# Front of a one-core hybrid encoder step: input blocks taken in threes, and the first B tile projected chunk by chunk behind the dt tile

## The chip, the core and the metric

The kernel runs on one core of one Trainium2 chip. The metric is the device time of the whole program in microseconds. The core's engines are TensorE (PE, matrix products and transposes), VectorE (DVE), ScalarE (ACT), GpSimd (POOL) and SyncE (SP), which issues the transfers. Each runs its own instructions in order, and they meet at semaphores.

## The reference, cut to what matters

The program is two layers over 1024 prompt tokens and 32 sample tokens of width 1024. Only the front of the even layer is touched:

```
h = rmsnorm(x, g_pre)                        # 1056 tokens, mean square over 1024
proj = einsum('bld,de->ble', h, w_in)        # columns: u, v, za, zb, xbc, dt_raw
xbc = silu(causal_dwconv(xbc))               # 12 tiles of 128 columns: x (8), B (2), C (2)
dt = softplus(dt_raw + dt_bias)              # 16 heads
acs = cumsum(dt * a)  per block of 128       # decays of the state recurrence
```

The recurrence, the gating branch, the output projection and the attention layer that follow are the same in both kernels.

## The kernel before, in words

**Layout.** The hidden state h is kept transposed: `HH` and `HL` are [128, 8, 1056], feature within tile, tile k, token. `HH` is h rounded to the matmul's input type and `HL` is the rest, so that a product is three matmuls: WH with HH, WH with HL, WL with HH. `WRAW`, `WH` and `WL` have two slots, so weight tile w uses slot w mod 2. A weight tile is loaded by SP into `WRAW`, rounded by ScalarE (`split_high`, to `WH`), and its rest is taken by GpSimd (`split_low`, to `WL`, counted by `w_low`). The tokens are projected in three chunks c of 352 columns, each into its own bank PB[c]. One chunk of one tile is 8 k-steps of 3 matmuls, 24 in all (`project_chunk`). ScalarE then reads the bank (`read_chunks`, counted by `c_read0` to `c_read2`), and only then may TensorE write the next tile's chunk there.

**Making h.** For each block of 128 tokens: a square with a row sum on ScalarE (L1127), the mean on VectorE (L1465), a root on ScalarE (L1134), a reciprocal and the scaling of the block in place on VectorE (L1482, L1466). TensorE transposes the scaled blocks (L643) in groups of four, four and one (`QUADS`) through four banks PB[3] to PB[6]. ScalarE writes HH from the bank (L1148), VectorE writes HL (L1469), and transposition i needs `h_lo` of transposition i - 4. In program order ScalarE does all nine squares and both first weight splits (`w = 0`, the dt tile, and `w = 1`, the first B tile) before the first HH. TensorE projects chunk 0 of the dt tile between the transposes of the second group, chunks 1 and 2 after the last HL, and then the four tiles of B and C.

**What follows.** When ScalarE has read the third dt chunk into the row buffer, VectorE and ScalarE pass the softplus of dt back and forth (`log1p_exp`, buffers `DTROW`). Then VectorE runs the convolution of the first B tile (`conv(0)`, buffer `ACC`) and the running sum of the decays (`ACSROW`), and ScalarE takes two exponentials. ScalarE comes to the second B tile only behind these:

```python
        for j in range(4):
            w = tile_no(W_BC, 1, j)
            if j > 0:
                act.wait_ge(S("conv"), j)
            read_chunks(w, parted(XR, 3, SAMP))
            ...
            if j == 0:
                act.wait_ge(S("dtc"), 3)
```

Of the kernel before, what the change touches and what calls it, by code (L numbers as in the profile page):

```python
# [11 lines left out]
P = 128  # L12
D = 1024
# [18 lines left out]
NEG = -30000.0  # L32
NEGBIG = -1e30
LN_EXP_SET = 6

W_DT, W_BC, W_XZ, W_V, W_UZ, W_OE, W_F, W_QKVZ, W_OO = 0, 1, 5, 21, 29, 45, 61, 62, 94
# [7 lines left out]
def tile_no(first, per, t):  # L45

    return first, per, t
# [46 lines left out]
def hybrid_trunk(nc, x_prompt, x_sample, cache_k, cache_v, cache_logf, state_ssd, state_conv,  # L94
# [63 lines left out]

    XS = at("XS", A_R3, [P, NB + 1, D])  # L160
    r = Region(A_R4, A_W)
    SQJ = r("SQJ", [P, D])
    ROWS = r("ROWS", [P, P])
    DEXP = r("DEXP", [8, 2, HP])
# [154 lines left out]
    def _(sp):  # L319
# [8 lines left out]
        for b in range(NB):  # L328
            sp.dma_start(XS[:, b, :], xp[:, b, :]).then_inc(S(f"x_in{b}"), 16)
            if b == 2:  # L330
                for src, (row, n) in (
                        (norm_pre[0].rearrange("(k p) -> k p", p=P), (PRE0, 8)),
                        (norm_post[0].rearrange("(k p) -> k p", p=P), (POST0, 8)),
                        (norm_pre[1].rearrange("(k p) -> k p", p=P), (PRE1, 8)),
                        (norm_post[1].rearrange("(k p) -> k p", p=P), (POST1, 8)),
                        (ssd_norm_g[0].rearrange("(k p) -> k p", p=P), (GSSD, 8)),
                        (conv_b[0].rearrange("(k p) -> k p", p=P), (CONVB, XBC_TILES)),
                        (gq[0:1, :], (GQ, 1)), (gk[0:1, :], (GK, 1)),
                        (state_conv[0, 0].rearrange("r (k p) -> (r k) p", p=P), (CTX, 36))):
# [12 lines left out]

# [284 lines left out]
    def _(pe):  # L637
# [11 lines left out]

        def project_chunk(w, u, c, hi, lo, start=True, stop=True, ready=None, ks=range(KT)):  # L650

            if c == 0:
                pe.wait_ge(S("w_low"), times(w, 1, 1))
            if start and not (isinstance(u[2], int) and u[0] + u[1] * u[2] == 0):
# [27 lines left out]
        first = tile_no(0, 1, 0)  # L682
# [401 lines left out]
    def _(act):  # L1084
# [33 lines left out]
                     (slice(two, CH), t[:, sample0:sample0 + DEC])]]  # L1118

        for b in range(NB + 2):
            if b <= NB:
                rows = sample_rows(b)
                act.wait_ge(S(f"x_in{b}"), 16)
                if b > 0:
                    act.wait_ge(S("x_ss"), b)
                act.activation(SQJ[0:rows, :], XS[0:rows, b, :], ACT.Square, accum_out=SS[0:rows, b:b + 1]) \  # L1127
                    .then_inc(S("x_ss"), 1)
            if b == 0:
                continue  # L1130
            b -= 1
# [3 lines left out]
            if b == 2:  # L1135
# [4 lines left out]
        order.fence()  # L1140
        act.wait_ge(S("w_clear"), 1)
        for w in range(2):
            split_high(tile_no(w, 1, 0))
        for q, (b0, nb, rows) in enumerate(QUADS):
            for k in range(KT):
                i = q * KT + k
                act.wait_ge(S("x_t"), i + 1)
                act.activation(HH[:, k, b0 * P:b0 * P + nb * rows], PB[3 + i % 4][:, 0:nb * rows], ACT.Copy,  # L1148
                               scale=COLS[:, PRE0 + k:PRE0 + k + 1]).then_inc(S("h_hi"), 1)

        def conv_silu(n, out):
            act.wait_ge(S("conv"), n + 1)
# [9 lines left out]
            order.fence()  # L1162
            act.activation(neg, lg, ACT.Exp, scale=-1.0).then_inc(S(name + "_a"), 1)

        read_chunks(tile_no(W_DT, 1, 0), whole(RW[4], HEADS_B), rows=HEADS_B)
        split_high(tile_no(W_DT + 2, 1, 0))
        load_ln_exp()
        log1p_exp_steps(RW[5][:, :], RW[6][:, :], RW[1][:, :], RW[2][:, :], "dtc")
        act.wait_ge(S("par_in"), 64)
        act.activation(EAL[0:HEADS_B, :], AL[0:HEADS_B, :], ACT.Exp).then_inc(S("dtc_a"), 1)  # L1170
        for j in range(4):
            w = tile_no(W_BC, 1, j)
            if j > 0:
                act.wait_ge(S("conv"), j)
            read_chunks(w, parted(XR, 3, SAMP))
# [282 lines left out]
    def _(dve):  # L1458
# [13 lines left out]
        for b in range(NB + 2):  # L1472
            if b <= NB:
                rows = sample_rows(b)
                dve.wait_ge(S("x_ss"), b + 1)
                ts(MS[0:rows, b:b + 1], SS[0:rows, b:b + 1], 1.0 / D, EPS, ALU.mult, ALU.add).then_inc(S("x_ms"), 1)
            if b == 0:
                continue
            b -= 1
# [5 lines left out]
            if b == 1:  # L1485
# [3 lines left out]
        for q, (b0, nb, rows) in enumerate(QUADS):  # L1489
            for k in range(KT):  # L1490
                i = q * KT + k
                cols = slice(b0 * P, b0 * P + nb * rows)
                dve.wait_ge(S("h_hi"), i + 1)
                stt(HL[:, k, cols], PB[3 + i % 4][:, 0:nb * rows], COLS[:, PRE0 + k:PRE0 + k + 1],
                    HH[:, k, cols].bitcast(f32), ALU.mult, ALU.subtract).then_inc(S("h_lo"), 1)

        def conv(n, tile, w):
            dve.wait_ge(S("c_read2"), times(w, 1, 1))
# [461 lines left out]
```

## Time and profile before

| | |
|---|---|
| time, median of 3 runs | 1733.57 us (1732.59 to 1736.33) |
| span of the profiled execution | 1733.1 us |
| TensorE busy | 1618.7 us, 93% |
| VectorE, ScalarE, GpSimd busy | 820.3, 639.0, 431.9 us |

The profiled execution has its span as its own time. It lies 0.5 us below the median of the runs. Busy time of TensorE is the time in which a matmul was in flight, and says nothing of its speed. A time in a row is counted from the span's start.

### The profile page before, as it was taken

The numbers are of one execution on the slowest core, as the hardware profiler recorded it, in microseconds if no ns is written. First come the engines' busy times: TensorE is split into PE (matmuls) and PEld (weight loads), VectorE is DVE, ScalarE is ACT, GpSimd is POOL, SyncE is SP. The second block draws the span as 40 slices with busy tenths as digits, with TensorE's granted clock in tenths as the row PEclk, the third lists the DMA queues.
The fourth block names the chain that finished last, engine by engine and source line by source line (L and its number), as shares of the span: only waits on it lengthen the run. The fifth ranks groups of instructions, "written<-read, shape, count | busy, mean of one in ns | idle before, by whom it ended". The sixth has DMA issues, their size and how long they took to land.

```text
span 1733.1 us, 27903 instructions
## 1 busy us (share of the span) xinstructions
PE 1618.7 (93%) x10174; PEld 1529.1 (88%) x10174; DVE 820.3 (47%) x1738; ACT 639.0 (37%) x1146; POOL 431.9 (25%) x261
## 2 busy tenths in 40 slices
PE   5899999998998999899997899999999999997995
PEld 4899999988998999799995788889888888986894
DVE  5745776674883122711117833443434344344426
ACT  6433332332224222511123344444444444444213
POOL 1113443451212121512211321211212121124113
PEclk9999999999999999899998999999999999998997
DMA  4121222112102111111140235523232332201103
GB/s 140 39 64 55 67 82 67 54 42 78 45 19 61 37 42 43 37 37 48 46 120 9 37 64 49 68 43 67 42 65 49 46 67 43 67 31 50 32 18 100
DMA packets 150349, 93.97 MB, mean 54 GB/s; under 512 B 8994, under 2 KB 144836, under 8 KB 150300
## 3 DMA queue, kind: packets, MB, share of 16 engines
q1 hardware_dynamic: 150300, 93.30, 23.5%
q8 instruction: 32, 0.52, 0.1%
q14 instruction: 17, 0.14, 0.0%
HBM read 78.95 MB, written 14.34 MB: 54 GB/s over the span
## 4 chain that ended last, share of the span: by engine, by line
PE 77%; DVE 8%; ACT 6%; issue 5%; POOL 1%; DMA 1%; SPq 0%; POOLq 0%; ACTq 0%; DVEq 0%
PE PB L639 72%; PE PB L643 5%; DVE NRML L1462 2%; DVE HX L1469 1%; ACT HH L1086 1%; ACT L1092 1%; DVE HL L1462 1%; ACT SB L1418 1%; DVE O L1462 1%; DMA XS<-in_x_prompt_dram 1%; ACT L1349 1%; ACT NRMH L1086 0%; DMA nf_rows<-NFROW 0%; DVE O L1469 0%; POOL HL L617 0%
## 5 line engine op out<-in xcount | busy, mean ns | idle before, releaser
L639 PE MATMUL PB<-HH,WH 128*128 128x352 f32 x2256 | 752.0, 333 | 36.3 <-DVE HL L1462 11.5
L639 PE MATMUL PB<-HH,WL 128*128 128x352 f32 x2256 | 731.9, 324 | 0.0
L639 PE MATMUL PB<-HL,WH 128*128 128x352 f32 x2256 | 731.5, 324 | 0.0
L639 PEld LDWEIGHTS PB<-HH,WH 128*128 128x128 f32 x2256 | 429.9, 191 | 60.2 <-issue 39.8
L519 POOL TENSOR_TENSOR WL<-WRAW,WH 128x1024 fp32r<-128x1024 f32 x102 | 249.4, 2446 | 771.1 <-ACT WH L1086 771.1
L639 PEld LDWEIGHTS PB<-HL,WH 128*128 128x128 f32 x2256 | 431.3, 191 | 0.0
L639 PEld LDWEIGHTS PB<-HH,WL 128*128 128x128 f32 x2256 | 430.0, 191 | 0.0
L1086 ACT ACTIVATE WH<-WRAW 128x1024 fp32r<-128x1024 f32 x102 | 107.4, 1054 | 90.0 <-PE PB L639 70.6
L1462 DVE TENSOR_TENSOR TMP<-O 128x352 f32 x48 | 25.2, 525 | 199.7 <-ACT O L1106 199.3
L1418 ACT ACTIVATE SB<-SB,small 128x128 f32<-128x128 f32 (+8 forms) x72 | 53.9, 748 | 81.7 <-DVE small L1466 81.6
L639 PE MATMUL PB<-PT,VTOK 128*128 128x128 f32 (+2 forms) x624 | 81.6, 274 | 0.1
L639 PEld LDWEIGHTS PB<-PT,VTOK 128*128 128x128 f32 (+1 forms) x624 | 78.1, 191 | 1.0 <-issue 0.2
L639 PE MATMUL PB<-KALL,QT 128*128 128x512 f32 (+4 forms) x208 | 78.7, 485 | 0.0
L1106 ACT ACTIVATE O<-PB 128x352 f32 (+1 forms) x48 | 22.1, 465 | 151.5 <-PE PB L639 150.6
L1462 DVE TENSOR_TENSOR Y<-PB,Y 128x128 f32 (+2 forms) x72 | 20.1, 280 | 116.6 <-PE PB L639 116.5
L1462 DVE TENSOR_TENSOR NRML<-NRM,NRMH 128x352 fp32r<-128x352 f32 x48 | 47.1, 980 | 59.1 <-ACT NRMH L1086 59.1
L547 POOL TENSOR_TENSOR M<-M,CBT 128x512 f32<-128x512 f32 (+1 forms) x48 | 62.2, 1321 | 34.2 <-ACT M L1228 34.2
L639 PE MATMUL PB<-YAH,WH 128*128 128x352 f32 x192 | 64.1, 334 | 3.4 <-DVE YAL L1462 3.4
L1462 DVE TENSOR_TENSOR UG<-UG,ZG 128x1056 f32<-128x1056 f32 x8 | 10.1, 1257 | 114.6 <-ACT ZG L1106 114.6
L1086 ACT ACTIVATE PT<-PB 128x512 f32<-128x512 f32 (+3 forms) x112 | 45.8, 447 | 47.3 <-PE PB L643 47.2
L639 PE MATMUL PB<-YAL,WH 128*128 128x352 f32 x192 | 62.6, 326 | 0.0
L639 PE MATMUL PB<-YAH,WL 128*128 128x352 f32 x192 | 62.5, 326 | 0.0
(239 smaller groups left out, 2060.3 us busy)
## 6 DMA issues: line engine op xcount, KB each, us to landing
WRAW<-in_w_in_even_dram SPq DMA_DIRECT2D x44, 512.0 KB, 3.8
WRAW<-in_w_in_odd_dram SPq DMA_DIRECT2D x32, 512.0 KB, 8.4
ACSB<-acs_rows SPq DMA_DIRECT2D x16, 528.0 KB, 4.8
XS<-in_x_prompt_dram SPq DMA_DIRECT2D x16, 512.0 KB, 6.2
WRAW<-in_w_out_even_dram SPq DMA_DIRECT2D x16, 512.0 KB, 3.9
NFB<-nf_rows SPq DMA_DIRECT2D x8, 656.0 KB, 3.9
out_dram<-VTOK SPq DMA_DIRECT2D x8, 512.0 KB, 3.2
out_dram<-KTOK SPq DMA_DIRECT2D x8, 512.0 KB, 3.0
```

Source lines behind the costliest of these rows:

```text
L519: pool.tensor_tensor(WL[:, slot(w), :, :], WRAW[:, slot(w), :, :], WH[:, slot(w), :, :].bitcast(f32), ALU.subtract).then_inc(S("w_low"), 1)
L547: pool.tensor_tensor(m, m, CBT[0:rows, g, b0:b0 + nb, 0:rows], ALU.mult).then_inc(S("m"), 1)
L639: return pe.matmul(out, lhsT, rhs, start=start, stop=stop)
L643: return pe.transpose(out, in_, IDENT[0:n, 0:n])
L1086: return act.activation(out, in_, ACT.Copy, scale=scale)
L1092: act.add_instruction(mybir.InstLoadActFuncSet(name=nc.get_next_instruction_name(), act_func_set_id=LN_EXP_SET, ins=[], outs=[]))
L1106: last = act.activation(out, PB[c][0:rows, cols], func)
L1349: act.activation(Y1[:, p, :], Y1[:, p, :], ACT.Silu).then_inc(S("zs"), 1)
L1418: act.activation(SB[0:rows, 0:width], SB[0:rows, 0:width], ACT.Exp, scale=SCALE, bias=NBIAS[0:rows, :], accum_out=RSUM[0:rows, :]).then_in ...
L1462: return dve.tensor_tensor(out, a, b, op)
L1469: return dve.scalar_tensor_tensor(out=out, in0=a, scalar=s, in1=b, op0=op0, op1=op1)
```

## The change

ScalarE and VectorE now take the input blocks three at a time: three squares, means and roots, then the HH and HL pieces of these three blocks, 384, 384 and 288 columns wide instead of 512, 512 and 32. TensorE transposes k-step k of a group of three and projects k-step k - 2 of the dt tile's chunk behind it. After each group it projects the same chunk of the first B tile. ScalarE rounds the dt tile before the first group's HH and the first B tile after it. It reads the chunks of both tiles as they come. The table set for the root is loaded once at the start. The load of the first B tile moves ahead of the last two prompt blocks, and small buffers move to where nothing early is overwritten.

```diff
+    FIRST_BLOCKS = ((0, 1, 2), (3, 4, 5), (6, 7, 8))
+    FIRST_COLS = (slice(0, 3 * P), slice(3 * P, 6 * P), slice(6 * P, TOK))
...
             if b == 3:
                 load_w(tile_no(W_DT, 1, 0), even(DT0, HEADS_B), HEADS_B)
+            if b == 5:
+                load_w(tile_no(W_BC, 1, 0), even(XBC0 + 8 * P))
...
-        for j in range(4):
+        for j in range(1, 4):
             load_w(tile_no(W_BC, 1, j), even(XBC0 + (8 + j) * P))
...
-        for q, (b0, nb, rows) in enumerate(QUADS):
-            pe.wait_ge(S("xn"), b0 + nb)
-            for k in range(KT):
-                i = q * KT + k
-                if i >= 4:
-                    pe.wait_ge(S("h_lo"), i - 3)
-                for j in range(nb):
-                    last = turn(PB[3 + i % 4][:, j * P:j * P + rows], XS[0:rows, b0 + j, k * P:(k + 1) * P])
-                last.then_inc(S("x_t"), 1)
-                if q == 1:
-
-                    project_chunk(first, first, 0, HH, HL, ks=[k])
-        pe.wait_ge(S("h_lo"), 24)
-        for c in (1, 2):
-            project_chunk(first, first, c, HH, HL)
-        for w in range(1, W_XZ):
+        def x_turn(tr, k):
+
+            i = 8 * tr + k
+            if k == 0:
+                pe.wait_ge(S("xn"), 3 * tr + 3)
+            if i >= 4:
+                pe.wait_ge(S("h_lo"), i - 3)
+            for j, b in enumerate(FIRST_BLOCKS[tr]):
+                rows = DEC if b == NB else P
+                last = turn(PB[3 + i % 4][:, j * P:j * P + rows], XS[0:rows, b, k * P:(k + 1) * P])
+            last.then_inc(S("x_t"), 1)
+
+        for tr in range(3):
+            for k in range(KT + 2):
+                if k < KT:
+                    x_turn(tr, k)
+                if k >= 2:
+                    pe.wait_ge(S("h_lo"), 8 * tr + k - 1)
+                    project_chunk(dt, dt, tr, HH, HL, ks=[k - 2])
+            if tr == 0:
+                pe.wait_ge(S("w_low"), W_BC + 1)
+            project_chunk(bc, bc, tr, HH, HL)
+        for w in range(W_BC + 1, W_XZ):
             project(tile_no(w, 1, 0), tile_no(w, 1, 0), HH, HL)
...
+        for tr in range(3):
+            b0 = 3 * tr
+            x_squares(b0)
+            x_squares(b0 + 1)
+            x_root(b0)
+            x_squares(b0 + 2)
+            x_root(b0 + 1)
+            x_root(b0 + 2)
+            if tr == 0:
                 act.wait_ge(S("rows_turn"), 1)
                 order(copy(COLS[:, :], PB[3][:, 0:N_ROWS]))
                 copy(DCOL[:, :], PB[3][:, P:P + 8]).then_inc(S("cols"), 1)
...
+                split_high(tile_no(W_DT, 1, 0))
+            if tr > 0:
+                first_chunk(0, tr - 1, whole(RW[4], HEADS_B), HEADS_B)
+            h_high(tr)
+            if tr == 0:
+                split_high(tile_no(W_BC, 1, 0))
+            else:
+                first_chunk(1, tr - 1, parted(XR, 3, SAMP))
...
-        read_chunks(tile_no(W_DT, 1, 0), whole(RW[4], HEADS_B), rows=HEADS_B)
+        first_chunk(0, 2, whole(RW[4], HEADS_B), HEADS_B)
         split_high(tile_no(W_DT + 2, 1, 0))
+        first_chunk(1, 2, parted(XR, 3, SAMP))
         load_ln_exp()
```

On TensorE, at the first transposes (`XS` is the token-major input, `WH`/`WL` the halves of the dt tile), before:

```order
L643 MATMUL PB<-IDENT,XS 128x128 [waits xn,cols]
L643 MATMUL PB<-IDENT,XS 128x128 x15
L643 MATMUL PB<-IDENT,XS 128x128 [waits h_lo]
L643 MATMUL PB<-IDENT,XS 128x128 x3
L643 MATMUL PB<-IDENT,XS 128x128 [waits h_lo]
```

At the same place after the change:

```order
L650 MATMUL PB<-IDENT,XS 128x128 [waits xn,cols]
L650 MATMUL PB<-IDENT,XS 128x128 x8
L646 MATMUL PB<-HH,WH 128x352 [waits w_low,h_lo]
L646 MATMUL PB<-HL,WH 128x352
L646 MATMUL PB<-HH,WL 128x352
L650 MATMUL PB<-IDENT,XS 128x128 x3
L646 MATMUL PB<-HH,WH 128x352 [waits h_lo]
```

The first projection stands behind nine transposes instead of forty, and it waits for the low half of its weights there.

On ScalarE, from the rounding of the weights to the first chunk reads (`DTROW` takes dt, `XR` the first B tile), before:

```order
L1134 ACTIVATE small<-small 32x1 [waits x_ms]
L1086 ACTIVATE WH<-WRAW 128x1024 [waits w_raw0,w_clear,act_order]
L1086 ACTIVATE WH<-WRAW 128x1024 [waits w_raw1]
L1148 ACTIVATE HH<-PB,COLS 128x512 [waits x_t] x16
L1148 ACTIVATE HH<-PB,COLS 128x32 [waits x_t] x8
L1106 ACTIVATE DTROW_93<-PB 16x352 [waits p_chunk] x3
L1086 ACTIVATE WH<-WRAW 128x1024 [waits p_chunk,w_raw0]
L1092 ACT_TABLE_LOAD
```

After the change, from the first group's rounding of the dt tile:

```order
L1101 ACTIVATE WH<-WRAW 128x1024 [waits w_raw0,w_clear,act_order]
L1156 ACTIVATE HH<-PB,COLS 128x384 [waits x_t] x8
L1101 ACTIVATE WH<-WRAW 128x1024 [waits w_raw1]
L1141 ACTIVATE SQJ,small<-XS 128x1024 [waits x_ss,x_in3]
L1141 ACTIVATE SQJ,small<-XS 128x1024 [waits x_ss,x_in4]
L1148 ACTIVATE small<-small 128x1 [waits x_ms]
L1141 ACTIVATE SQJ,small<-XS 128x1024 [waits x_ss,x_in5]
```

The rounding of the first B tile now follows the first group's eight HH pieces, and the next group's squares follow that. Further on, behind the last HH pieces:

```order
L1101 ACTIVATE DTROW_93<-PB 16x352 [waits p_chunk]
L1101 ACTIVATE WH<-WRAW 128x1024 [waits p_chunk,w_raw0]
L1101 ACTIVATE XR<-PB 128x320 [waits p_chunk]
L1101 ACTIVATE XR<-PB 128x32
L1107 ACT_TABLE_LOAD
L1199 ACTIVATE DTROW_95<-DTROW_94 16x1056 [waits dtc]
```

The read of the first B tile's last chunk now stands ahead of the table load that the softplus of dt needs.

## Rows read from the trace of the kernel before

**Rows 1.** The page's head and its line of busy times.

```profile
span 1733.1 us, 27903 instructions
...
PE 1618.7 (93%) x10174; PEld 1529.1 (88%) x10174; DVE 820.3 (47%) x1738; ACT 639.0 (37%) x1146; POOL 431.9 (25%) x261
```

**Rows 2.** Waits of TensorE in the whole span: total, times, longest, in us.

```profile
PE PB L639 <- ACT XR L1106: 6.0, 1, 6.0
```

**Rows 3.** The chain that ended last, 36 to 80 us: start, length, what.

```profile
37.70 9.54 PE PB L639 x48
47.26 0.46 ACT DTROW L1106
...
52.65 1.09 ACT DTROW L1159
...
60.57 3.35 DVE ACC L1469
...
69.85 2.36 DVE ACSROW L1554
...
75.63 0.35 ACT XR L1106
```

**Rows 4.** Timeline of TensorE, 13 to 35 us: start, length, instructions.

```profile
14.95 3.65 PE L643 MATMUL PB<-IDENT,XS 128*128 128x128 f32 x16 [3.70 <-DVE XS L1466]
23.39 4.45 PE L643 MATMUL PB<-IDENT,XS 128*128 128x128 f32 x20 [4.80 <-DVE HL L1469]
27.58 0.43 PE L639 MATMUL PB<-HH,WH 128*128 128x352 f32 x1
...
28.17 0.60 PE L643 MATMUL PB<-IDENT,XS 128*128 128x128 f32 x4
...
29.09 0.60 PE L643 MATMUL PB<-IDENT,XS 128*128 128x128 f32 x4
```

**Rows 5.** Windows: length, PE busy (instructions), four other engines, then PEclk.

```profile
37.80:41.20 3.40, 3.40 (x12) 3.40 (x13) 0.00 (x0) 0.00 (x0) 0.00 (x0) 0.51 0.01 2
...
47.26:70.10 22.84, 22.84 (x144) 22.59 (x142) 20.22 (x20) 11.95 (x16) 5.27 (x2) 1.00 0.16 47
...
76.12:82.20 6.08, 6.08 (x21) 6.08 (x22) 5.97 (x9) 2.83 (x5) 2.87 (x1) 0.50 0.04 7
```

**Rows 6.** Timeline of ScalarE, 7 to 9 us.

```profile
7.19 1.28 ACT L1134 ACT_TABLE_LOAD   x1
8.48 0.20 ACT L1134 ACTIVATE small<-small 128x1 f32<-128x1 f32 x1
8.59 1.04 ACT L1127 ACTIVATE SQJ<-XS 128x1024 f32<-128x1024 f32 x1
```

**Rows 7.** Groups by shape, 0 to 48 us: busy, mean ns of one | idle before.

```profile
L1469 DVE SCALAR_TENSOR_TENSOR HL<-PB,COLS,HH 128x512 fp32r<-128x512 f32 x16 | 11.7, 749 | 2.5 <-ACT HH L1148 2.2
...
L1148 ACT ACTIVATE HH<-PB,COLS 128x512 fp32r<-128x512 f32 x16 | 10.7, 685 | 2.5 <-PE PB L643 2.4
...
L1466 DVE TENSOR_SCALAR XS<-XS,small 128x1024 f32<-128x1024 f32 x8 | 6.0, 753 | 0.3
...
L519 POOL TENSOR_TENSOR WL<-WRAW,WH 128x1024 fp32r<-128x1024 f32 x2 | 5.0, 2524 | 18.3 <-ACT WH L1086 18.3
L1086 ACT ACTIVATE WH<-WRAW 128x1024 fp32r<-128x1024 f32 x3 | 3.0, 1040 | 0.0
L1148 ACT ACTIVATE HH<-PB,COLS 128x32 fp32r<-128x32 f32 x8 | 1.8, 287 | 0.6 <-PE PB L643 0.5
L1469 DVE SCALAR_TENSOR_TENSOR HL<-PB,COLS,HH 128x32 fp32r<-128x32 f32 x8 | 1.6, 247 | 0.3 <-ACT HH L1148 0.2
```

**Rows 8.** Timeline of the DMA queue, 3 to 8 us: issue, length.

```profile
5.94 0.43 SPq L323 DMA_DIRECT2D WRAW<-in_w_in_even_dram  x1
```

**Rows 9.** DMA issues, 0 to 30 us: KB each, median us from issue to landing.

```profile
WRAW<-in_w_in_even_dram SPq DMA_DIRECT2D x1, 64.0 KB, 4.7
```

**Rows 10.** Timeline of GpSimd, 46 to 62 us.

```profile
60.28 2.51 POOL L519 TENSOR_TENSOR WL<-WRAW,WH 128x1024 fp32r<-128x1024 f32 x1 [8.78 <-ACT WH L1086]
```

More of the change, by code:

```diff
@@ L34 @@
 LN_EXP_SET = 6
+SQRT_SET = 3
 W_DT, W_BC, W_XZ, W_V, W_UZ, W_OE, W_F, W_QKVZ, W_OO = 0, 1, 5, 21, 29, 45, 61, 62, 94
@@ L160, in hybrid_trunk @@
     XS = at("XS", A_R3, [P, NB + 1, D])
-    r = Region(A_R4, A_W)
+    r = Region(A_R5, A_R5 + 4 * TOK * 4)
     SQJ = r("SQJ", [P, D])
@@ L650, in project_chunk @@
         def project_chunk(w, u, c, hi, lo, start=True, stop=True, ready=None, ks=range(KT)):
-            if c == 0:
+            if c == 0 and ks[0] == 0:
                 pe.wait_ge(S("w_low"), times(w, 1, 1))
-            if start and not (isinstance(u[2], int) and u[0] + u[1] * u[2] == 0):
+            if start and ks[0] == 0 and not (isinstance(u[2], int) and u[0] + u[1] * u[2] == 0):
                 pe.wait_ge(S(f"c_read{c}"), times(u, 1, 0))
@@ L681, in _ @@
         pe.wait_ge(S("cols"), 1)
-        first = tile_no(0, 1, 0)
-        for q, (b0, nb, rows) in enumerate(QUADS):
-            pe.wait_ge(S("xn"), b0 + nb)
-            for k in range(KT):
-                i = q * KT + k
-                if i >= 4:
-                    pe.wait_ge(S("h_lo"), i - 3)
-                for j in range(nb):
-                    last = turn(PB[3 + i % 4][:, j * P:j * P + rows], XS[0:rows, b0 + j, k * P:(k + 1) * P])
-                last.then_inc(S("x_t"), 1)
-                if q == 1:
-                    project_chunk(first, first, 0, HH, HL, ks=[k])
-        pe.wait_ge(S("h_lo"), 24)
-        for c in (1, 2):
-            project_chunk(first, first, c, HH, HL)
-        for w in range(1, W_XZ):
+        dt, bc = tile_no(W_DT, 1, 0), tile_no(W_BC, 1, 0)
+        def x_turn(tr, k):
[19 more added lines that the diff above has]
+        for w in range(W_BC + 1, W_XZ):
             project(tile_no(w, 1, 0), tile_no(w, 1, 0), HH, HL)
@@ L1118, in parted, with x_squares, x_root @@
                      (slice(two, CH), t[:, sample0:sample0 + DEC])]]
[L1121 to L1131, printed above, removed]
+        def x_squares(b):
+            rows = sample_rows(b)
+            act.wait_ge(S(f"x_in{b}"), 16)
+            wait(act, "x_ss", b)
+            act.activation(SQJ[0:rows, :], XS[0:rows, b, :], ACT.Square, accum_out=SS[0:rows, b:b + 1]) \
+                .then_inc(S("x_ss"), 1)
+        def x_root(b):
             rows = sample_rows(b)
@@ L1134, in _, with h_high, first_chunk @@
             act.activation(RT[0:rows, b:b + 1], MS[0:rows, b:b + 1], ACT.Sqrt).then_inc(S("x_rt"), 1)
-            if b == 2:
+        def h_high(tr):
+            cols = FIRST_COLS[tr]
+            for k in range(KT):
+                i = 8 * tr + k
+                act.wait_ge(S("x_t"), i + 1)
+                act.activation(HH[:, k, cols], PB[3 + i % 4][:, 0:cols.stop - cols.start], ACT.Copy,
+                               scale=COLS[:, PRE0 + k:PRE0 + k + 1]).then_inc(S("h_hi"), 1)
+        def first_chunk(n, c, outs, rows=P):
+            act.wait_ge(S("p_chunk"), 2 * c + n + 1)
+            for cols, out in outs[c]:
+                last = copy(out, PB[c][0:rows, cols])
+            last.then_inc(S(f"c_read{c}"), 1)
+        act.add_instruction(mybir.InstLoadActFuncSet(name=nc.get_next_instruction_name(),
+                                                     act_func_set_id=SQRT_SET, ins=[], outs=[]))
+        for tr in range(3):
[7 more added lines that the diff above has]
+            if tr == 0:
                 act.wait_ge(S("rows_turn"), 1)
@@ L1139, in _ @@
                 copy(DCOL[:, :], PB[3][:, P:P + 8]).then_inc(S("cols"), 1)
[L1140 to L1149, printed above, removed]
+                order.fence()
+                act.wait_ge(S("w_clear"), 1)
+                split_high(tile_no(W_DT, 1, 0))
[6 more added lines that the diff above has]
+                first_chunk(1, tr - 1, parted(XR, 3, SAMP))
         def conv_silu(n, out):
@@ L1174, in _ @@
                 act.wait_ge(S("conv"), j)
[L1175 removed]
+                read_chunks(w, parted(XR, 3, SAMP))
             split_high(tile_no(W_BC + 2, 1, j))
@@ L1471, in _, with x_mean, x_normalised @@
         order(dve.memset(ONES[:, :], 1.0))
[L1472 to L1479, printed above, removed]
+        def x_mean(b):
+            rows = sample_rows(b)
+            dve.wait_ge(S("x_ss"), b + 1)
+            ts(MS[0:rows, b:b + 1], SS[0:rows, b:b + 1], 1.0 / D, EPS, ALU.mult, ALU.add).then_inc(S("x_ms"), 1)
+        def x_normalised(b):
             rows = sample_rows(b)
@@ L1484, in _ @@
             ts(XS[0:rows, b, :], XS[0:rows, b, :], RR[0:rows, b:b + 1], None, ALU.mult).then_inc(S("xn"), 1)
-            if b == 1:
+        for tr in range(3):
+            b0 = 3 * tr
+            x_mean(b0)
+            x_mean(b0 + 1)
+            x_normalised(b0)
+            x_mean(b0 + 2)
+            x_normalised(b0 + 1)
+            if tr == 0:
                 dve.wait_ge(S("rows_in"), 160)
@@ L1488, in _ @@
                     .then_inc(S("dexp"), 1)
-        for q, (b0, nb, rows) in enumerate(QUADS):
+            x_normalised(b0 + 2)
+            cols = FIRST_COLS[tr]
             for k in range(KT):
-                i = q * KT + k
-                cols = slice(b0 * P, b0 * P + nb * rows)
+                i = 8 * tr + k
                 dve.wait_ge(S("h_hi"), i + 1)
-                stt(HL[:, k, cols], PB[3 + i % 4][:, 0:nb * rows], COLS[:, PRE0 + k:PRE0 + k + 1],
+                stt(HL[:, k, cols], PB[3 + i % 4][:, 0:cols.stop - cols.start], COLS[:, PRE0 + k:PRE0 + k + 1],
                     HH[:, k, cols].bitcast(f32), ALU.mult, ALU.subtract).then_inc(S("h_lo"), 1)
```

## The prediction

> **What bounds the kernel now.** I read the head of the page first [rows 1]: 1733.1 us, TensorE busy for 93% of it. So a gain must come from a place where TensorE waits, or runs slowly, and this change touches only the first 80 us. Next I read who made TensorE wait [rows 2]. One wait of 6.0 us has ScalarE's reads into XR behind it. Then I followed the chain that ended last through that stretch [rows 3]. It tells more than the wait does. TensorE ends the dt tile's chunks 1 and 2 at 37.70 + 9.54 = 47.24. From 47.26 the chain leaves TensorE: ScalarE reads dt, then come the softplus on both engines (its first exponential at 52.65), the convolution of the first B tile (60.57), the running sum (69.85), the exponentials, and at 75.63 the read of the second B tile's first chunk. TensorE resumes at 76.12. I call the end of the dt tile's last chunk T. From T to the resumption it is 76.12 - 47.24 = 28.9 us of serial VectorE and ScalarE work. In its shadow TensorE has two tiles, 144 matmuls in 22.84 us [rows 5], and then stands for 6.0 us.
>
> So the question is not how early TensorE has its work done. It is when the last dt chunk is done. Work of TensorE done before T costs time, and the same work after T is free while the 6.0 us of slack last.
>
> **What the change moves.** Chunks 0 and 1 of the first B tile go from behind T to ahead of it. At 22.84 / 144 = 0.16 us each, their 48 matmuls are 7.6 us. Behind T only 8 + 24 k-steps (96 matmuls, 15.2 us) are left, so the stall at 76 grows from 6.0 to some 13.5 us; that costs nothing by itself. Against the 7.6 us stands what the front gains. TensorE now stands idle between its first 16 transposes and the next, 4.80 us before 23.39 [rows 4], because ScalarE does all squares and two roundings first. With threes this start comes forward. I worked out T group by group.
>
> *Group 1.* The dt weights are issued at 5.94 [rows 8] and land 4.7 us later [rows 9], at 10.6. The copies of the gain columns lie near there too. The rounding (1.04) and the low half (2.52) [rows 7] then end at 10.8 + 1.04 + 2.52 = 14.4. Before, this latency was covered by the squares; now TensorE has nine transposes (1.9 us) and then waits for it. The removed table load (1.28, [rows 6]) brings the third block's normalisation forward, but 14.4 is later than that anyway, so the removal is worth nothing here. Ahead of TensorE lie 15 transposes and 24 matmuls: 1.7 + 3.8 = 5.5 us at full clock. It has just idled, so I let 3 us of it run at half, +1.5, and the last steps wait for HH and HL of the eighth transpose, +0.7. The dt chunk ends near 22.1, ScalarE's last HH at 20.7. Now comes the first B tile's rounding and low half: 20.7 + 1.04 + 0.1 + 2.5 = 24.4. TensorE waits 2.3 us. Its 24 matmuls then take 3.8 us, with some 3 us at half again +1.4: 29.6.
>
> *Group 2.* The squares of blocks 3 to 5 end in the shadow of that wait (each 1.04 and 0.1 to 0.2 for its row sum, [rows 6]; scaling 0.75, [rows 7]): 21.7 + 3 x 1.2 + 0.4 = 25.7, and scaled by 27.4. Group 2 starts at 29.6. Nine transposes take 1.0, and the first matmul waits for a transpose, an HH and an HL, 29.6 + 0.6 + 0.6 + 0.6 = 31.4. Then 24 matmuls and 15 transposes, 3.8 + 1.7, with 0.7 of waits at the end: 37.6. The B chunk ends at 41.4.
>
> *Group 3.* ScalarE has its last HH of group 2 at 36.3, reads a chunk and then does the squares of blocks 6 to 8: 36.7 + 3 x 1.2 + 0.5 = 40.8. VectorE has two blocks to scale then (each 0.75 and a reciprocal) and ends at 42.4. TensorE stands 1.0 us. First matmul 42.4 + 1.7 = 44.1, then 24 matmuls and five more k-steps of transposes (0.29 each), 3.8 + 1.4, and 0.6 of waits: T = 49.9.
>
> So T moves from 47.24 to 49.9, +2.7 us. Behind T one step is added to the chain: ScalarE's read of the B chunk (T + 3.9 + 0.5) and then the table load (1.28) end at T + 5.7, and the exponential that started at T + 5.4 (52.65) starts 0.3 us late. A page of the Trainium skill, "ScalarE: Activation LUTs", section "What ACT_TABLE_LOAD costs", adds a drain of some 1.38 us to each load. By that the exponential would be 1.7 us late and the sum 1.4 us higher; the row here has the next activation at 8.48, straight behind the load, so I leave it out.
>
> Two moves cancel. GpSimd's low half at 60.28 [rows 10] lies over the first convolution pass that took 3.35 us [rows 3]. Now it starts about 1.7 us earlier after T and meets a product of the softplus instead: one slowed step either way, 0 to +0.3. The B weights ahead of blocks 6 and 7 delay those by 1 to 2 us, and they are not needed before 36.7. Everything behind the resumption keeps its distances.
>
> Sum: 2.7 + 0.3 + 0.2 for these = +3.2 us, 0.18%. The span is 0.5 us below the median; laid on the median it gives 1736.8. About 0.2%, 3.5 us, is what a measurement of this kernel can tell from no change, so the likeliest case lies just at that bound.
>
> **The rivals.**
>
> *The clock costs more, slower.* TensorE now pauses ahead of all three groups. The half clock lasted 3.4 us in one place and 6.1 in another (12 and 21 matmuls, [rows 5]). One more stretch of each kind before T costs half its length, 1.7 or 3.0: +4.9 to +6.2, 1738.5 to 1740. Against it: from 28.17 on the mixed transposes and matmuls ran at full clock [rows 4]. The skill's page "TensorE: Matmul & The Clock Gate", Part 4, says that transposes do not count as activity as matmuls do. By that rule the groups would stay at half for longer, 3 us or more each. The trace speaks against it: after 20 transposes alone the spacing halved at 27.58. Chance 0.2.
>
> *The orders balance, no change.* If TensorE gets to full clock at once in group 1 (-1.5) and the B tile's halves are there 1 us sooner, T is 47.4 and the total +0.2 to +1: 1734. Chance 0.17.
>
> *Faster.* The pipeline has no waits at all. From 14.4 to T there are 63 transposes (8 of them small) and 120 matmuls, 6.6 + 19.1 = 25.7 us, so T = 40 to 43 and the time 1727 to 1730. It decides if T comes before 43.5. What speaks against it is the low half of the first B tile at 24.4, which follows from the order on ScalarE. Another way to this side: that the stall at 76 is not bound by the dt chain but by TensorE's own work. Then finishing the B tile earlier would pay up to 4 us. The chain [rows 3] has no TensorE piece between 47.24 and 76.12, which denies it. Chance 0.08.
>
> *As worked out*, +1.5 to +5: 0.55.
>
> **How the numbers follow.** The forecast is the likeliest case, 1736.8. Its own range is 1735 to 1738.6. The range over all is 1733.2 to 1740.3: it takes in the balance and nearly all of the clock case, and leaves out the fast case and a small tail. Slower by over 0.2% (above 1737.04): the clock case and 0.24 of the likeliest, 0.44. Within 0.2%: the balance and 0.31 of the likeliest, 0.48. Faster: 0.08.
>
> **What would show it.** In the changed kernel's timeline: the first dt matmul near 14.4, waiting for GpSimd; the first B matmul near 24.4, waiting for it again; the last dt chunk ending near 50; the first exponential of dt at T + 5.7; and a stall of some 13 us that ends at T + 29.2. I am wrong if T is below 46 or above 53, if the distance from T to the resumption is not 29 to 29.5, or if the stall at 76 shrinks.

## The result, and the profile after the change

The changed kernel takes 1747.06 us (median of 4 runs, 1744.53 to 1747.53) against 1734.04 (4 runs, 1732.59 to 1736.33): ratio 1.0073, 95% interval 1.0061 to 1.0085. It is 13.0 us slower; the forecast was 3.2 us slower (1736.8), with 1740.3 at the end of its range. The page's head stands against [rows 1]:

```profile
span 1745.7 us, 27896 instructions
...
PE 1621.4 (93%) x10174; PEld 1526.0 (87%) x10174; DVE 817.4 (47%) x1738; ACT 638.1 (37%) x1145; POOL 432.4 (25%) x261
```

Work hardly changed (TensorE's busy time grew by 2.7 us), so most of the 12.6 us of span are waiting. The waits of TensorE in the first 60 us of the changed kernel (total, times, longest) show one that no step of the forecast has:

```profile
PE PB L646 <- ACT DTROW L1101: 7.1, 2, 3.9
PE PB L646 <- POOL WL L526: 2.1, 1, 2.1
```

TensorE waits twice for ScalarE's read of a dt chunk. The chain that ended last, 24 to 92 us (start, length, what), says where:

```profile
26.19 1.16 ACT SQJ L1141 x2
...
27.77 0.35 ACT DTROW L1101
28.12 0.14 issue
28.25 5.45 PE PB L646 x24
33.70 0.34 PE PB L650 x3
...
43.03 1.16 ACT SQJ L1141 x2
...
44.59 0.35 ACT DTROW L1101
44.94 0.04 issue
44.98 5.62 PE PB L646 x24
...
57.58 1.90 PE PB L646 x9
59.51 0.46 ACT DTROW L1101
...
64.14 0.53 ACT XR L1101 x2
64.68 1.28 ACT L1107
65.98 1.10 ACT DTROW L1199
...
89.03 0.35 ACT XR L1121
89.39 0.14 issue
89.52 2.69 PE PB L646 x8
```

Read it from the bottom. TensorE resumes at 89.52 instead of 76.12 [rows 3], 13.4 us later, which is the whole loss and a little more. T, the end of the dt tile's last chunk, is 59.5 instead of 47.26, so 12.25 of the 13.4 us are T. Above it stand the two places: each of the first two B chunks (x24) follows a read of dt, and that read follows the squares (`SQJ`) of the *next* group. The B chunk is written to the bank PB[c] from which ScalarE must first read the dt chunk, and in program order that read stands behind three squares and three roots. ScalarE's timeline behind the first group:

```profile
22.77 1.05 ACT L1101 ACTIVATE WH<-WRAW 128x1024 fp32r<-128x1024 f32 x1
23.72 1.05 ACT L1141 ACTIVATE SQJ<-XS 128x1024 f32<-128x1024 f32 x1
...
27.67 0.44 ACT L1101 ACTIVATE DTROW<-PB 16x352 f32<-16x352 f32 x1
```

TensorE had the dt chunk done at 28.25 - 3.92 = 24.33, and the read begins at 27.67.

Windows over the two B chunks and the third group of the changed kernel (length, PE busy and instructions, four other engines, PEclk) show a second thing. The B chunks, each right behind a wait, ran partly at half clock and took 5.3 to 5.5 us where 24 matmuls at full clock take 3.8. The third group ran at full clock and still needed 7.4 us from its first matmul, where the forecast had 5.8:

```profile
28.20:33.50 5.30, 5.25 (x24) 5.28 (x25) 1.04 (x3) 0.00 (x0) 0.00 (x0) 0.71 0.24 72
44.90:50.40 5.50, 5.42 (x24) 5.42 (x25) 1.16 (x3) 0.03 (x1) 0.00 (x0) 0.69 0.00 0
52.10:59.50 7.40, 7.33 (x39) 5.62 (x39) 3.63 (x8) 3.36 (x7) 0.00 (x0) 1.00 0.00 0
```

### The profile page after: what moved, and what is told of

Read it like the earlier page. It is cut to its first block, busy times and chain, and to the rows that moved or that the text cites. A ratio compares the mean times of both kernels' runs of the same rounds, so it can differ in the third digit from the quotient of the medians.

```text
span 1745.7 us, 27896 instructions
## 1 busy us (share of the span) xinstructions
PE 1621.4 (93%) x10174; PEld 1526.0 (87%) x10174; DVE 817.4 (47%) x1738; ACT 638.1 (37%) x1145; POOL 432.4 (25%) x261
## 4 chain that ended last, share of the span: by engine, by line
PE 77%; DVE 8%; ACT 6%; issue 5%; POOL 1%; DMA 1%; SPq 0%; POOLq 0%; ACTq 0%; DVEq 0%
PE PB L646 71%; PE PB L650 5%; DVE NRML L1503 2%; DVE HX L1510 1%; ACT HH L1101 1%; ACT L1107 1%; ACT SB L1459 1%; DVE HL L1503 1%; DMA WRAW<-in_w_in_even_dram 1%; DVE O L1503 1%; ACT L1390 1%; ACT NRMH L1101 0%; DMA nf_rows<-NFROW 0%; ACT WH L1101 0%; DVE O L1510 0%
```

## The experiments

**One table first.** T is the start of ScalarE's read of the third dt chunk, "back" the time at which TensorE resumes behind the stall. The last column is worked out: 1734.0 + (back - 76.12).

| kernel | T | back | time, median | from "back" |
|---|---|---|---|---|
| before | 47.26 | 76.12 | 1734.0 | |
| changed | 59.51 | 89.52 | 1747.1 | 1747.4 |
| B chunks in their own banks | 51.34 | 80.56 | 1739.3 | 1738.4 |
| the same, full rows | 50.20 | 79.42 | 1738.3 | 1737.3 |
| dt read ahead of the squares | 58.36 | 88.38 | 1746.6 | 1746.3 |
| the same, full rows | 51.48 | 81.50 | 1741.3 | 1739.4 |
| changed, full rows | 60.07 | 90.14 | 1747.5 | 1748.0 |
| threes, B tile behind dt | 55.59 | 84.45 | 1742.1 | 1742.3 |
| the same, full rows | 50.94 | 79.79 | 1737.9 | 1737.7 |
| threes, B tile behind dt, squares first | 51.49 | 80.45 | 1738.2 | 1738.3 |
| before, chunk 1 between sample transposes | 46.93 | 75.78 | 1733.2 | 1733.7 |

In nine of these ten the median lies within 1 us of what the resumption gives; the tenth misses by 1.9. So the forecast's frame, time goes one to one with the end of the dt chain, holds. What differs is T. How exactly it holds, the table makes look better than it is. T and "back" come from one execution each, and that one lies up to 3.8 us from the median of its kernel (1751.3 against 1747.5 for the changed kernel with full rows, 1735.6 against 1738.3 for own banks with full rows). An execution's own time less its "back" is 1656.1 to 1661.2 us, so from a single profile the frame is good to some 2.5 us either way. (The span of a profiled execution is 1.8 us below its own time in all these kernels, 1745.7 and 1747.53 for the changed one; the front had only the median to set it against.)

The ratios below are against runs of the kernel before that were taken beside each kernel; their medians are 1733.8 to 1734.8 us. The other three kernels, in section 5, change ScalarE's order ahead of "back" itself, so they have no row here.

**1. The bank.** The first B tile's chunks go to banks 7, 0 and 1 instead of 0, 1 and 2; the order of work on ScalarE stays.

```diff
+    B_BANK = (7, 0, 1)
...
             if tr == 0:
                 pe.wait_ge(S("w_low"), W_BC + 1)
+            else:
+                pe.wait_ge(S(f"c_read{tr - 1}"), 1)
```

> The changed kernel, with one thing undone: the first B tile's chunks go to the banks 7, 0 and 1, so that they don't wait until ScalarE has read the dt chunk out of the same bank. Theory A (the shared bank: the B chunk waits for a ScalarE read that stands behind the next group's three squares): the first B chunk starts at 26.3 us, when its low half is there, instead of 28.25; group 2 follows at 31.6; the second B chunk follows the dt chunk without a pause; the squares of group 3 start at 38.4 and the last dt chunk ends (T) near 53.2 instead of 59.47. Time near 1740.3. Rival B (the pauses come from the squares themselves and the bank wait only fills them): T stays above 57, time above 1744.5.

Measured: 1739.3 us (1738.51 to 1740.53, 7 runs), ratio 1.0032 (1.0020 to 1.0043). The tile's matmuls and reads take their bank from this table, and the second B tile waits for the reads of banks 0 and 1. Of the 13.0 us, 7.8 are gone with a change of bank. The waits of TensorE in the first 60 us no longer name `DTROW`:

```profile
PE PB L647 <- POOL WL L527: 3.1, 2, 2.0
PE PB L651 <- DVE XS L1522: 1.3, 2, 0.7
```

In the trace T is 8.2 us earlier, but 2.2 of these lie ahead of the first B chunk, in the first group, which the edit doesn't touch; 6.0 are behind it. Most of the 6.0 are three pieces: the first chunk's wait falls from 3.92 to 1.99 us (what is left is the wait for its low half), the second's from 3.22 to nothing, and the second chunk, with no pause ahead of it, takes 3.8 us at full clock instead of 5.5. With the 2.2 us taken off, theory A's times come out to 0.3 us (first B chunk 24.10, third group's end 51.34, against 26.3 and 53.2), and rival B, T above 57, is out. So the bank is worth 6.0 us by the one trace and 7.8 by the medians.

**2. The order on ScalarE.** The same wait attacked from the other side: the bank stays, ScalarE reads the dt chunk ahead of the next squares.

```diff
-            if tr > 0:
-                first_chunk(0, tr - 1, whole(RW[4], HEADS_B), HEADS_B)
             h_high(tr)
...
                 split_high(tile_no(W_BC, 1, 0))
+            if tr < 2:
+                first_chunk(0, tr, whole(RW[4], HEADS_B), HEADS_B)
```

> The changed kernel with one move: ScalarE reads the dt tile's chunk 0 (and 1) straight behind its group's last HH piece, ahead of the next group's three squares, instead of behind them. Bank PB[0] is then free when the first B chunk wants it, as with a bank of its own, but the read itself waits for TensorE's chunk and holds the squares of the next group up. Theory (the price of the change is the wait for the read of the shared bank): the first B chunk starts 2 us or more earlier (near 26 instead of 28.25), the 3.2 us wait at 44.98 is gone or shrinks below 1, T (the end of the dt tile's last chunk) comes near 54 instead of 59.5, and the time is 1741 to 1743. Rival (the queue on ScalarE is the price, wherever the read stands): the squares of the next group end later by what the B chunk gains, T stays above 57 and the time above 1744.5.

Measured: 1746.55 us (1743.79 to 1748.34), ratio 1.0066 (1.0051 to 1.0081). The rival had the time and not the mechanism. The wait is gone (0.54 us is left) and the third group starts 5.3 us earlier than in the changed kernel, at 45.16 instead of 50.44. Then it takes 13.2 us instead of 9.1. This group's window and a piece of TensorE's timeline:

```profile
45.10:58.30 13.20, 13.09 (x48) 9.81 (x48) 4.15 (x10) 4.37 (x9) 0.00 (x0) 0.61 0.00 1
```

```profile
45.16 1.70 PE L650 MATMUL PB<-IDENT,XS 128*128 128x128 f32 x9 [1.33 <-DVE XS L1507]
...
49.50 0.87 PE L650 MATMUL PB<-IDENT,XS 128*128 128x128 f32 x3
50.30 0.66 PE L646 MATMUL PB<-HH,WH 128*128 128x352 f32 x1
...
51.34 0.87 PE L650 MATMUL PB<-IDENT,XS 128*128 128x128 f32 x3
```

A k-step takes 1.85 us, the spacing of half clock, from 47.35 on to 57.6. The group had started at full clock, behind a wait of 1.33 us, and fell 2.2 us later. The next kernel's third group was at half clock too, from its start.

**3. The B tile wholly behind the dt tile**, so that only the threes are left; and with it all squares first, as before the change.

```diff
-            if tr == 0:
-                pe.wait_ge(S("w_low"), W_BC + 1)
-            project_chunk(bc, bc, tr, HH, HL)
-        for w in range(W_BC + 1, W_XZ):
+        for w in range(W_BC, W_XZ):
```

> The changed kernel, with the first B tile projected wholly behind the dt tile's third chunk, as before; blocks still in threes. Theory A: without the B chunks T falls to the serial order on ScalarE (squares of a group only behind the HH pieces of the last): group 2 at 29.3, group 3 at 41.9, T near 51.0, resumption of TensorE 28.9 us after T; time near 1738, still slower than before by 3.8 us. Rival C (the B chunks ahead of T are the whole loss, and the threes alone are worth a gain): T at or below 47.2, time at or below 1733.6.

> As e3_b_behind, and ScalarE and VectorE take all nine blocks' squares, roots and scalings and both weight roundings first, as before; only the transposes and the dt projection go in threes. Theory A: the pauses between groups are gone, T near 48.8 (first dt matmul at 23.7, group 2 at 31.7, group 3 at 39.8), time near 1735.5. If the pipelining behind each group is worth something by itself, T is below 47.2 and the time below 1733.5.

Measured: 1742.13 us (1739.99 to 1745.35), ratio 1.0040 (1.0025 to 1.0055), and with the squares first 1738.21 (1736.52 to 1741.44), ratio 1.0024 (1.0014 to 1.0035). Both miss, by 4.1 and 2.7 us. Rival C, that the threes alone are a gain, is out: T is 55.59, not 47.2, and neither kernel is faster than before. In the first kernel TensorE waits 5.0 and 4.0 us ahead of groups 2 and 3, and group 3 is at half clock nearly from end to end (40.78 to 55.4). With the squares first, the first dt matmul waits until 25.4 for a low half behind squares that end 1.5 us later than before (21.5 against 20.0). The B weights are loaded ahead of blocks 6 and 7 there, and ScalarE waits 2.0 us for block 6, where it had waited 0.25. The forecast put the delay by that load at nothing, which holds only while the squares of blocks 6 to 8 come late.

**4. The shape of the sample block's transposes.** In the changed kernel's third group a step of three transposes and three matmuls takes 1.08 us at full clock; in its second group it takes 0.81. The difference is that the third transpose has 32 rows. TensorE's weight loads in one such step of the changed kernel:

```profile
53.64 0.30 PEld L650 LDWEIGHTS PB<-IDENT,XS 128*128 128x128 f32 x2
54.11 0.13 PEld L650 LDWEIGHTS PB<-IDENT,XS 32*128 32x128 f32 x1 [0.17 <-issue]
54.28 0.19 PEld L646 LDWEIGHTS PB<-HH,WH 128*128 128x128 f32 x1
```

The small load waits 0.17 us for nothing that the profile shows, and the next one follows after another 0.17, where loads between full transposes stand 0.11 apart. So four kernels got one edit: GpSimd writes zeros over the sample block, and it is transposed with all 128 rows. The result of the 96 added rows is never read. The load of the sample rows, and the small loads behind it, wait for the zeros.

```diff
+        pool.memset(XS[:, NB, :], 0.0).then_inc(S("x_clear"), 1)
...
-                rows = DEC if b == NB else P
-                last = turn(PB[3 + i % 4][:, j * P:j * P + rows], XS[0:rows, b, k * P:(k + 1) * P])
+                last = turn(PB[3 + i % 4][:, j * P:j * P + P], XS[:, b, k * P:(k + 1) * P])
```

On the kernel with its own banks:

> The kernel in which the first B tile's chunks have banks of their own, and in it the last block of the third group (32 sample tokens) is transposed with all 128 rows, 96 of them zeros that GpSimd writes first; the added columns of the bank aren't read. Theory (the 32-row transposes hold up the loading of weights): a k-step of the third group, three transposes and three matmuls, falls from 1.08 us to the 0.81 us of the second group, T comes 1.5 to 2 us earlier (51.3 to near 49.5), and the time falls from 1739.3 to 1737.4. Rival (the step is set by the way from the transpose over ScalarE's HH piece and VectorE's HL piece back to TensorE): the step stays at 1.05 us or more, and the time at 1739 to 1739.7.

Measured: 1738.25 us (1735.54 to 1739.36, 11 runs), ratio 1.0020 (1.0011 to 1.0029). The step is 0.81 us, as in the theory. T is 1.1 us earlier, less than the 1.5 to 2 expected, since TensorE now waits 0.49 us for an HL piece behind the nine transposes. The time is 1.0 us less, and the two intervals overlap, so the gain in time isn't clear of noise here. From its timeline of TensorE:

```profile
44.53 0.49 PE L653 MATMUL PB<-IDENT,XS 128*128 128x128 f32 x3
...
45.34 0.49 PE L653 MATMUL PB<-IDENT,XS 128*128 128x128 f32 x3
```

On the kernel that reads dt first, and on the threes with the B tile behind:

> The changed kernel with the dt chunk read ahead of the next squares, in which the third group ran ten microseconds at half clock (1.85 us a k-step), and with the sample block transposed with all 128 rows, 96 of them zeros, as one further edit. Theory (the 32-row transposes leave TensorE idle in each k-step, and with that it doesn't get back to full clock): PEclk returns to 1.00 within the first steps of the third group, its steps take 0.81 us there, T comes at 52.5 to 54 instead of 58.3, and the time is 1740 to 1742 instead of 1746.5. Rival (the shape only adds its 0.27 us a step at full clock, and the half clock comes from the pause ahead of the group): the third group stays at half clock, with steps near 1.5 us, T at 56 to 57 and the time at 1744 to 1745.5.

> The kernel in threes with the whole B tile behind the dt tile (which took 1742.1, its third group at half clock throughout), and the sample block transposed with all 128 rows as the one further edit. Theory (the gaps of the 32-row transposes held the clock down there): the third group starts near 40.8 at half clock and rises within its first two or three steps, T at 48.5 to 50.5 instead of 55.6, the time at 1735.5 to 1737.5. That would leave the threes by themselves 1.5 to 3.5 us behind the kernel before. Rival (the pause of 4 us ahead of the group, not the shape, held it down): half clock throughout, steps of 1.5 us, T at 53 to 54, the time at 1740 to 1741.

Measured: 1741.32 us (1739.66 to 1743.87), 5.2 less than without the edit, and 1737.85 (1735.98 to 1741.58, 10 runs), 4.3 less; the second is 0.4 us outside what its theory gave. The window of the third group in the kernel that reads dt first:

```profile
43.50:51.40 7.90, 7.31 (x48) 6.30 (x48) 3.97 (x9) 4.14 (x9) 0.00 (x0) 1.00 0.00 0
```

7.9 us and a clock of 1.00, where it had been 13.2 and 0.61. In the other kernel TensorE comes out of its 4.0 us wait at half clock again, and is back at full clock 4.4 us after the group's start (41.67 to 46.09); without the edit the window 40.7 to 55.6 has a mean of 0.51. Both pairs say the same, and the time ranges of the first pair hardly touch. Not all of its gap is the shape's: 1.6 of the 6.9 us of T lie ahead of the third group, where the two executions had a different stretch of half clock. At the full-clock price of 0.27 us a step the shape is worth 1.2 us of the third group; the rest of the 5.3 us there is the clock.

How the shape acts on the clock stays open. The third groups of the changed kernel, of the one with own banks and of the one with squares first have the same 32-row transposes and ran at a clock of 1.00 from end to end, so these transposes don't pull it down wherever they stand. And each trace is one execution. A page of the Trainium skill, "TensorE: Matmul & The Clock Gate", Part 4, says that a transpose doesn't count as busy in the way a matmul does. The pairs neither confirm nor refute it, since a step with full rows is also a shorter step between the same matmuls.

On the changed kernel itself:

> The changed kernel as it is, with the sample block transposed with all 128 rows as the one edit. Theory (the shape's price in the change as made is 0.27 us a k-step at full clock, since its third group ran at full clock): steps of 0.81 instead of 1.08 us, T at 57.4 to 57.9 instead of 59.5, the time at 1745 to 1745.6, with the waits of 3.9 and 3.2 us for the bank unchanged. Rival (a step that is shorter only moves the wait to the HH and HL pieces): T above 59, time above 1746.5.

Measured: 1747.50 us (1746.57 to 1751.3), no gain. Time and T are the rival's, its mechanism is not: the waits for HL pieces grew from 0.7 to 1.2 us only. The profiled execution is the slowest of the four, 3.8 us above their median. In it the third group did get shorter, 7.9 instead of 9.1 us, but started 1.7 us later, since both B chunks stayed longer at half clock. The windows of the B chunks:

```profile
27.70:34.50 6.80, 6.75 (x25) 6.76 (x26) 1.04 (x3) 0.00 (x0) 0.00 (x0) 0.54 0.20 60
45.90:52.10 6.20, 6.16 (x24) 6.17 (x25) 1.11 (x3) 0.00 (x0) 0.00 (x0) 0.59 0.00 0
```

All that the edit puts ahead of the first of them is the writing of zeros on GpSimd, and the first dt matmul is not later for it (14.99 against 15.29). So a B chunk behind these pauses cost 1.5 to 3 us more than at full clock, and the amount differed although TensorE's instructions up to there were the same. Here a saving of 1.2 us can't be seen under that.

**5. The other end of the chain, and the kernel before made better.** The second B tile is read ahead of the two decay exponentials; chunk 1 of dt is projected between the sample block's transposes; and both together, with the two roundings moved into places where ScalarE waits.

```diff
             read_chunks(w, parted(XR, 3, SAMP))
-            split_high(tile_no(W_BC + 2, 1, j))
-            conv_silu(j, (BT, CT)[j // 2][:, j % 2, :])
-            if j == 0:
+            if j == 1:
                 act.wait_ge(S("dtc"), 3)
                 order(act.activation(RW[5][:, :], RW[5][:, :], ACT.Exp))
                 act.activation(RW[3][:, :], ACSROW[:, :], ACT.Exp).then_inc(S("dtc_a"), 1)
+            split_high(tile_no(W_BC + 2, 1, j))
+            conv_silu(j, (BT, CT)[j // 2][:, j % 2, :])
```

> The kernel before, with one move: ScalarE reads the second B tile out of its banks ahead of the two exponentials of the decays, not behind them. If the stall of TensorE before 76 us is this order on ScalarE alone (my chain from T to the resumption), TensorE goes on at 70.1 without a pause; the next wait, for the read behind the second convolution, then lets the fourth B/C tile start near 86.1 instead of 90.7, less what a slower clock behind that new pause costs: time 2 to 4.6 us below before, 1729.5 to 1732. If the chain through the convolutions decides anyway, no change.

```diff
-                if q == 1:
+                if q > 0:
 
-                    project_chunk(first, first, 0, HH, HL, ks=[k])
+                    project_chunk(first, first, q - 1, HH, HL, ks=[k])
```

> The kernel before with one move: the dt tile's chunk 1 is projected k-step by k-step between the transposes of the sample block, instead of behind all of them. Theory (time goes 1:1 with T, by whatever T moves): the sample block's eight transposes stand before in a stretch in which TensorE waits for HH and HL of 32 columns, some 3 us, and the stretch behind runs 3.4 us at half clock. With matmuls between them T moves from 47.24 to 43 to 44.5 and the time to 1730 to 1731.5. Rival (time does not follow T one to one when T moves earlier, since something else of the chain, the running sum or the second B tile's read, is bound elsewhere): T moves, and the time stays above 1732.5.

```diff
             if b == 2:
...
+                act.wait_ge(S("w_clear"), 1)
+                split_high(tile_no(W_DT, 1, 0))
         order.fence()
-        act.wait_ge(S("w_clear"), 1)
-        for w in range(2):
-            split_high(tile_no(w, 1, 0))
         for q, (b0, nb, rows) in enumerate(QUADS):
+            if q == 2:
+                split_high(tile_no(W_BC, 1, 0))
```

> The kernel before with chunk 1 of dt between the sample block's transposes, and two further moves on ScalarE: the dt tile's rounding stands in ScalarE's wait for the fourth block instead of behind all squares, the first B tile's rounding behind the second group's HH pieces, and the second B tile is read ahead of the two decay exponentials. Theory: the first four-block group's HH pieces start 2.1 us earlier, T comes at 40.7 to 42, the read order adds its 1.5 to 2 us, and the time is 1725.5 to 1728. Rival (the first group is bound by the squares and the scaling, not by the roundings): T as with chunk 1 alone, and the time 1728.5 to 1730.

> The kernel before with the three moves that gave 1728.5 (chunk 1 of dt between the sample block's transposes, the roundings placed where ScalarE waits, the second B tile read ahead of the two exponentials), and the sample block transposed with all 128 rows. Theory (each 32-row transpose between matmuls costs TensorE 0.37 us where its matmul-only k-step takes 0.48, a full one 0.11): eight times 0.26 is 2.1 us or a little more, T comes at 41.2 to 41.8 instead of 43.9, and the time is 1726 to 1726.7. Rival (the loop over HH and HL of the sample block, 0.29 and 0.25 us a step, or their semaphores, bind there): T stays above 43.3 and the time at 1728 to 1729.

Measured: the read order alone 1732.05 us, ratio 0.9989 (0.9980 to 0.9998); chunk 1 alone 1733.23, ratio 0.9991 (0.9982 to 1.0000); together 1728.47 (1726.49 to 1730.71, 5 runs), ratio 0.9965 (0.9951 to 0.9979); with full rows 1728.64, ratio 0.9961 (0.9947 to 0.9974). The read order did what was expected of it: TensorE doesn't stand at 76 us any more, its next wait, of 4.8 us, ends at 86.32 (86.1 expected), and the 2.0 us gained are at the small end of the forecast. Chunk 1 alone missed: T moved by 0.3 us and not by 3. No half clock was left in that stretch, but each small transpose between matmuls cost 0.37 us, as in the chain of the combined kernel:

```profile
32.98 0.17 PE PB L643
33.16 0.68 PE PB L639 x3
...
43.93 0.46 ACT DTROW L1105
```

0.85 us a step, where three matmuls alone take 0.48. With full rows a step took 0.59. The eight steps gained 2.1 us, and T only 0.6 (43.33 against 43.93), mostly because in that execution TensorE was 1.2 us later when the steps began: it rose from half clock later. The medians show no gain either, so T and time are its rival's, though its step fell as in the theory. The combined kernel missed as well, 43.93 against 40.7 to 42 for T and 1728.47 at the edge of its rival. Its 6.1 us (against 1734.61 beside it) are a T that is 3.3 us earlier, some 2 of the read order, and 0.8 that I can't place. No kernel here is faster, and it takes the blocks in fours.

## Why the prediction was wrong, step by step

*The frame held.* The chain [rows 3], time one to one with T, the stall that grows without costing (14.0 us against the 13 forecast) and the direction were right. Two of its three signs of being wrong came: T above 53 (59.5), and a distance from T to the resumption outside 29 to 29.5 (30.0).

*The step that failed:* "Nine transposes take 1.0 [...] The B chunk ends at 41.4", and the same for the first group: each B chunk was laid directly behind the dt chunk, with the low half of its weights as the only wait. The rule that I had written down in the front, that TensorE may write the next tile's chunk only when ScalarE has read the bank, was not applied to the moved chunks, and the read's place behind the next squares was not looked up in the order. In place of a start at 24.4 behind the low half, the first B chunk started at 28.25 behind ScalarE's read, and the second, forecast without a pause, waited 3.22 us. The kernel with own banks shows the price: 6 us of T, 7.8 us of time.

The error in T is 59.5 - 49.9 = 9.6 us. By the trace of the changed kernel it splits like this:

| step | forecast | measured | adds |
|---|---|---|---|
| first dt matmul | 14.4 | 15.29 | 0.9 |
| dt chunk 0 to its end | 7.7 us | 9.04 | 1.3 |
| wait ahead of B chunk 0 | 2.3 | 3.92 | 1.6 |
| B chunk 0 | 5.2 | 5.3 | 0.1 |
| group 2 to the end of dt chunk 1 | 8.0 | 8.2 | 0.2 |
| wait ahead of B chunk 1 | 0 | 3.22 | 3.2 |
| B chunk 1 | 3.8 | 5.46 | 1.7 |
| wait ahead of group 3 | 1.0 | 0 | -1.0 |
| group 3 to T | 7.5 | 9.07 | 1.6 |

The two waits are 4.8, and the half clock of B chunk 1 (1.7), which comes straight behind its wait, belongs to them. Not all of the first wait is the bank's: the low half was there at 26.26 and not at 24.4, so with its own bank the chunk would still have waited 1.9 us. The first two rows are sizes: the dt weights were rounded at 11.65 and not 10.8, and group 1 stayed at a half-clock spacing (0.29 us a matmul) for 5.6 us where I had allowed 3; the clock column shows 1.00 there, as it did at 23 to 27 us before. The last row is the small transpose: I gave each k-step of group 3 three equal transposes, 0.29 + 0.48 us, and it took 1.08. [Rows 7] price the sample block's HH and HL pieces, but no row of its transposes on TensorE was read.

*Behind T*, +0.3 was forecast and +1.15 came (30.01 against 28.86 us): the last B chunk waited 0.5 us for its bank too, so its read ended at T + 5.2 and the first exponential started at T + 6.5 instead of T + 5.7. The table load itself took 1.28 us with the exponential straight behind it (64.68, 65.98), so the extra drain of the Trainium skill's page "ScalarE: Activation LUTs", section "What ACT_TABLE_LOAD costs", does not show here either, and leaving it out was right.

*"Work of TensorE done before T costs time"* was too simple. The kernel with B chunks ahead in their own banks and full rows takes 1738.25 us, the one with all of B behind 1737.85. The chunks fill waits of 5.0 and 4.0 us that TensorE has in threes anyway, so what they cost is what they exceed them by. The threes alone cost some 4 us; the B chunks, done well, next to nothing more. Read from these kernels in turn, the 13.0 us are some 8 for the bank, 1 for the small transposes (not clear of noise) and 4 for the threes.

*The rival on the clock* was right in kind, extra half clock behind each pause, and its price of 1.7 to 3.0 us a stretch was near the 1.5 to 3.0 measured. It was added to a sum that lacked the bank, so 1747 lay outside its range as well.

## What to carry to other kernels

When work is moved up on one engine, list for each moved instruction every semaphore that it waits for, and find in the other engine's order what now stands ahead of the instruction that signals it; a bank's reader counts like an operand's writer. A pause of TensorE can be paid twice, by its length and by the half clock behind it: here half clock followed each of the waits of 3.2 to 5.0 us ahead of a group or a chunk. So a wait moved to a place with matmuls on the critical path can cost more than it shows. Give a small remainder block the shape of its neighbours if it sits in the middle of a TensorE stream.

## What the runs showed of the hardware

- A 32-row transpose between matmuls took 0.37 us, a 128-row one 0.11: a step of three matmuls and one transpose 0.85 against 0.59, of three and three 1.08 against 0.81.
- Two kernels with such transposes stayed at half clock for 10 and some 14 us with TensorE never waiting for another engine. With full rows the first stream was at full clock throughout, and the second rose to it after 4.4 us. Three other kernels in threes had such transposes in a group at full clock throughout. That the gaps at the small weight loads keep a low clock down is my reading of it. It wasn't shown apart from the shape.
- The length of a half-clock stretch isn't fixed: the first B chunk behind the same wait of 3.92 us took 5.3 us in the changed kernel (28.25 to 33.54) and 6.7 in the one with full rows (27.75 to 34.49).
- GpSimd's low half slows a VectorE product with two inputs in SBUF. The two timelines of the changed kernel at that place:

```profile
71.15 2.50 POOL L526 TENSOR_TENSOR WL<-WRAW,WH 128x1024 fp32r<-128x1024 f32 x1 [7.40 <-ACT WH L1101]
```

```profile
70.13 4.62 DVE L1503 TENSOR_TENSOR DTROW<-DTROW,DTROW 16x1056 f32<-16x1056 f32 x2 [0.32 <-ACT small L1211]
```

Two products that take 1.25 us each alone took 4.62 together, and the convolution passes behind them were spared (4.04 us for three). The page "SBUF — State Buffer" of the Trainium skill, section "SBUF: two separate sides", describes this as an exclusive lock; the second product, which starts at 71.41 just behind the low half's start and ends at 74.75, some 1.1 us after the low half's end at 73.65, agrees with it. So the slowed step only changed its place, and the forecast's "two moves cancel" was right.
